# Attention projection of a hybrid encoder: two pairs of token tiles as seven 256-wide products each, with sums of rows kept in the residual tiles

## The reference

```python
h = rms_norm(x, norm_mix_g[l])
u = jnp.einsum('bsd,dc->bsc', h, w_in)         # one projection for four mixers
u_na, u_ml, u_cv, u_at = jnp.split(u, [...], axis=-1)
# u_at: 512 columns: 256 of queries (4 heads), 128 of keys and 128 of values (2 heads)
qd = axial_rope(rms_norm(qd, att_q_norm_g), seq)
kd = axial_rope(rms_norm(kd, att_k_norm_g), seq)
o_at = blocked_gqa(qd, kd, vd)
# ... three other mixers, gates, branch projections, W_out, then x += that
x = x + hierarchical_moe(rms_norm(x, norm_ffn_g[l]), ...)
```

## Time and profile before

| what | value |
|---|---|
| median of 3 runs | 2052.47 us (2051.21 to 2052.56) |
| the profiled execution's own time | 2054.26 us |
| its span (first to last instruction) | 2052.4 us |
| mean granted TensorE clock | 0.986 of full speed |
| PE busy | 1962.9 us, 96% |
| DVE, ACT, POOL busy | 1057.4, 530.5, 388.9 us |
| PE's share of the chain that ended last | 81% |
| head of the first layer, until PE begins the `cv` products | 59.92 us |
| head of the second layer, from PE's first transpose | 1024.88 to 1074.96 us |

### The profile page before, as it was taken

The page is one execution under the profiler, slowest core; times in us unless marked ns, Lnnn a source line. Parts: engine busy times, 40 slices in busy tenths (PEclk is TensorE's granted clock), DMA queues, the critical chain, the costliest instruction groups (busy, mean ns, idle before and its releaser), DMA issues.

```text
span 2052.4 us, 24577 instructions
## 1 busy us (share of the span) xinstructions
PE 1962.9 (96%) x8928; PEld 1263.0 (62%) x8928; DVE 1057.4 (52%) x1895; ACT 530.5 (26%) x1128; POOL 388.9 (19%) x298
## 2 busy tenths in 40 slices
PE   8999999999999999999699999999999999989994
PEld 4555657655556545888445556676656655458882
DVE  3588606554455876111455884255545468651116
ACT  3234312344440001111122332133453300111112
POOL 2322223122120002000323222232112100120013
PEclk9999999999999999999899999999999999999997
DMA  5455668122316505999841111111222183169896
GB/s 212 183 206 200 252 235 319 66 77 88 124 62 250 219 21 215 391 383 375 304 145 74 73 72 72 71 53 62 78 98 108 66 320 145 42 245 424 356 382 243
DMA packets 73400, 375.20 MB, mean 183 GB/s; under 512 B 6289, under 2 KB 8721, under 8 KB 60066
## 3 DMA queue, kind: packets, MB, share of 16 engines
q1 hardware_dynamic: 40818, 259.27, 32.7%
q10 hardware_dynamic: 23824, 82.90, 10.5%
q0 software_dynamic: 8640, 31.46, 4.0%
HBM read 262.41 MB, written 112.25 MB: 183 GB/s over the span
## 4 chain that ended last, share of the span: by engine, by line
PE 81%; DVE 7%; DMA 4%; ACT 3%; issue 2%; POOL 2%; ACTq 0%; DVEq 0%; SPq 0%; POOLq 0%
PE bank L817 35%; PE bank L1761 9%; PE bank L1621 8%; PE bank L1646 5%; PE bank L1796 4%; PE bank L830 3%; PE bank L595 2%; PE bank L795 2%; PE bank L848 2%; PE bank L871 2%; PE bank L927 2%; PE bank L857 2%; DMA blocks<-ring,slots 1%; PE bank L1753 1%; PE bank L912 1%
## 5 line engine op out<-in xcount | busy, mean ns | idle before, releaser
L817 PE MATMUL bank<-hT,ring 128*128 128x384 f32 x1056 | 361.4, 492 | 5.5 <-ACT gbuf L1008 5.5
L817 PE MATMUL bank<-x,ring 128*128 128x384 f32 x1056 | 360.7, 490 | 3.8 <-issue 2.6
L817 PEld LDWEIGHTS bank<-hT,ring 128*128 128x128 f32 x1056 | 196.6, 191 | 152.7 <-issue 31.0
L817 PEld LDWEIGHTS bank<-x,ring 128*128 128x128 f32 x1056 | 194.9, 190 | 146.7 <-issue 26.6
L1187 DVE SCALAR_TENSOR_TENSOR reg_a<-cvx,pp,reg_a 128x783 f32<-128x783 f32 x120 | 141.2, 1177 | 4.3
L981 ACT ACTIVATE sums<-bank 128x384 f32<-128x384 f32 x132 | 64.7, 490 | 289.4 <-PE bank L817 286.9
L1148 DVE SCALAR_TENSOR_TENSOR gbuf<-bank,sums 128x384 f32<-128x384 f32 x96 | 53.5, 558 | 138.5 <-PE bank L817 106.0
L2152 DVE SCALAR_TENSOR_TENSOR prob<-prob,bank 128x256 f32<-128x256 f32 x30 | 12.6, 421 | 180.1 <-ACT prob L1873 180.0
L595 PE MATMUL bank<-ring,hT 128*128 128x512 f32 x192 | 89.2, 620 | 1.6 <-ACT hT L614 1.6
L1841 ACT ACTIVATE prob<-x 128x1024 f32<-128x1024 f32 x12 | 12.7, 1057 | 291.8 <-DVE x L2004 291.8
L1402 POOL TENSOR_TENSOR ring<-cvx,ring 128x512 f32<-128x512 f32 x20 | 25.6, 1282 | 304.8 <-PE bank L817 304.8
(11 more groups left out here) (332 smaller groups left out, 3212.7 us busy)
## 6 DMA issues: line engine op xcount, KB each, us to landing
ring<-in_wd SPq DMA_DIRECT2D x26, 2048.0 KB, 8.5
blocks<-hT SPq DMA_DIRECT2D x16, 3072.0 KB, 20.5
gate_dram<-gbuf ACTq DMA_DIRECT2D x64, 384.0 KB, 2.4
ring<-gate_dram SPq DMA_DIRECT2D x16, 1536.0 KB, 7.6
ring<-in_we SPq DMA_DIRECT2D x8, 2048.0 KB, 13.6
hT<-blocks ACTq DMA_DIRECT2D x26, 512.0 KB, 9.0
wide<-in_we SPq DMA_DIRECT2D x6, 2048.0 KB, 20.2
oT<-in_we SPq DMA_DIRECT2D x6, 2048.0 KB, 18.1
```

Source lines behind the costliest of these rows:

```text
L817: mm = nc.tensor.matmul(bank[i % 2][:, 0:HALF], w[:, k, :], a[:, k, :], start=(k == 0 and r in (0, 1, 3)), stop=(k == 3), skip_group_check ...
```

## The change

Tiles 1 and 2, and tiles 4 and 5, are projected as pairs (`AT_PAIRS`), each in seven products: here the weights' column halves of 256 are what moves, a product has four matmuls of 256 columns (new L629), and r = 0 to 6 take the blocks in the order b11, b21, T2, D, T3, b22, T4. Tiles 0 and 3 stay as they were (new L612). Four sums of weights (D, T2, T3, T4; `weights_sum`, new L760, 128 x 1024 each) are made by DVE into `wide`, four sums of rows for each pair (`rows_sum`, new L769, 128 x 512 each) into the tiles of `x` of the pair itself, once they are scaled. The load of the bias table to `wide` goes behind the second chunk load of `mix_sync`. ACT copies products 0, 2, 3 and 6, DVE adds 1, 4 and 5 (new L777). The sums of rows of the whole for `cv` now wait until product 5 of the second pair is done, since they are written over all of `x`, and piece 2 of part 0 of the rotation stands between the second and the third of them; the other pieces move as well. POOL's powers of the tiles all come ahead of that of the rotation.

```diff
-PROJ_UNITS = {"at": 6, "mo": 6, "mg": 2}
+PROJ_UNITS = {"mo": 6, "mg": 2}
+AT_PAIRS = (1, 4)
...
-    for u in range(PROJ_UNITS["at"]):
-        add("proj", "at", u)
-    add("rope", 1, 0)
+    for t in range(T):
+        if t in AT_PAIRS:
+            for r in range(PRODUCTS):
+                add("proj", "at", t, r)
+        elif t - 1 not in AT_PAIRS:
+            add("proj", "at", t, None)
     for i in range(2 * PRODUCTS):
         product("cv", i // PRODUCTS, i % PRODUCTS)
-        if i in (1, 5):
-            add("rope", 1, 1 + i // 5)
-        if i == 5:
+        if i == 1:
+            add("rope", 0, 3)
+        if i in (2, 4, 6):
+            add("rope", 1, i // 2 - 1)
+        if i == 6:
             add("rope", 1, 3)
...
+            def pair(t, r):
+                i = at["proj", "at", t, r]
+                if r < 2:
+                    pe.wait_ge(ht_ev, 2 * t + 1 + r)
+                else:
+                    pe.wait_ge(s_done, 4 * AT_PAIRS.index(t) + {2: 2, 3: 2, 4: 3, 5: 4, 6: 4}[r])
+                if r == 6:
+                    pe.wait_ge(ht_ev, 2 * t + 4)
+                if i >= 2:
+                    pe.wait_ge(proj_ev[i % 2], i // 2)
+                b, a = ((at_b11, at_q(t, 0)), (at_b21, at_q(t, 1)), (at_t2, at_s(t, 1)), (at_d, at_s(t, 0)),
+                        (at_t3, at_s(t, 2)), (at_b22, at_s(t, 3)), (at_t4, at_q(t + 1, 1)))[r]
+                for k in range(4):
+                    mm = nc.tensor.matmul(bank[i % 2][:, 0:BW], a[:, k, :], b[:, k, :], start=(k == 0 and r in (0, 1, 3)),
+                                          stop=(k == 3), skip_group_check=True)
+                mm.then_inc(proj_mm, 1)
+
+            turn(0)
+            for first in AT_PAIRS:
+                tile(first - 1)
+                turn(first + 1)
+                for r in range(PRODUCTS):
+                    if r == 5 and first + 2 < T:
+                        turn(first + 2)
+                    pair(first, r)
...
             head_square(act, layer, 1)
-            for t in range(1, T):
-                if t + 1 < T:
-                    head_square(act, layer, t + 1)
-                evict(t)
-                project(t - 1)
-            project(T - 1)
+            head_square(act, layer, 2)
+            evict(1)
+            project(0)
+            evict(2)
+            head_square(act, layer, 3)
+            head_square(act, layer, 4)
+            for r in (0, 2, 3):
+                pair(1, r)
+            evict(3)
+            pair(1, 6)
+            head_square(act, layer, 5)
+            evict(4)
+            project(3)
+            evict(5)
+            for r in (0, 2, 3, 6):
+                pair(4, r)
...
+            if layer:
+                for n in range(4):
+                    weights_sum(n)
+                add_late(0)
+                variance(0)
+                scale(0)
+                add_late(1)
+                add_late(2)
+            else:
+                norm(0)
+            norm(1)
+            norm(2)
             if layer == 0:
-                for t in range(T - 1):
-                    variance(t)
-                    scale(t)
...
+                weights_sum(0)
+                weights_sum(1)
+            rows_sum(1, 0)
+            rows_sum(1, 1)
+            pair(1, 1)
+            for n in (2, 3):
+                if layer == 0:
+                    weights_sum(n)
+                rows_sum(1, n)
+            norm(3)
+            pair(1, 4)
+            pair(1, 5)
             dve.wait_ge(consts_done, 16)
             dve.wait_ge(params_in, 32 * (layer + 1))
             rope(dve, done, 0, 0)
-            variance(T - 1)
-            scale(T - 1)
-            for piece in (1, 2, 3):
-                rope(dve, done, 0, piece)
+            norm(4)
+            norm(5)
+            rows_sum(4, 0)
+            rows_sum(4, 1)
+            pair(4, 1)
+            rows_sum(4, 2)
+            rows_sum(4, 3)
+            rope(dve, done, 0, 1)
+            pair(4, 4)
+            pair(4, 5)
             done(ts_(bg_half, pp[:, PP_BG:PP_BG + 32], 0.5, None, ALU.mult), bgh_done)
...
                 if r == 2:
-                    pe.wait_ge(s_done, 4)
+                    pe.wait_ge(s_done, 4 * len(AT_PAIRS) + 4)
...
-            dve.wait_ge(ht_ev, 2 * T)
+            dve.wait_ge(proj_mm, at["proj", "at", AT_PAIRS[-1], PRODUCTS - 2] + 1)
+            done.n[s_done.num] = 4 * len(AT_PAIRS)
             done(tt(s_of[0], quarter[1][0], quarter[1][1], ALU.add), s_done)
             done(tt(s_of[1], s_of[0], quarter[0][0], ALU.subtract), s_done)
+            rope(dve, done, 0, 2)
             done(tt(s_of[2], quarter[0][0], quarter[1][0], ALU.subtract), s_done)
             done(tt(s_of[3], quarter[0][1], s_of[1], ALU.subtract), s_done)
```

More of the change, by code:

```diff
@@ L581, in head_tensor, with tile @@
             pe.wait_ge(ident_in, 16)
-            turn(0)
-            for t in range(T):
+            def tile(t):
+                i = at["proj", "at", t, None]
                 for k in range(KD):
@@ new lines, in pair, with norm @@
+            def pair(t, r):
+                i = at["proj", "at", t, r]
+                dve.wait_ge(proj_mm, i + 1)
+                held = i - 3 if r == 5 else i - 1
+                dve.wait_ge(proj_ev[held % 2], held // 2 + 1)
+                to = {1: atr[:, t, 0:BW], 4: atr[:, t + 1, BW:], 5: atr[:, t, BW:]}[r]
+                tt(to, bank[i % 2][:, 0:BW], sums[:, 1 if r == 5 else 0, 0:BW], ALU.add).then_inc(proj_ev[i % 2], 1)
+                dve.wait_ge(proj_ev[i % 2], i // 2 + 1)
+            def norm(t):
+                variance(t)
+                scale(t)
+                if layer and t + 2 < T:
+                    add_late(t + 2)
```

84 lines of the change are left out of this document (53 added, 31 removed).

## The result

| | before | after |
|---|---|---|
| median of 4 runs of each on one chip | 2052.51 us (2051.21 to 2052.90) | 2067.01 us (2066.81 to 2067.56) |
| the profiled execution: its time, its span | 2054.26, 2052.4 | 2066.81, 2065.0 |
| mean granted TensorE clock | 0.986 | 0.983 |
| PE, DVE, POOL busy | 1962.9, 1057.4, 388.9 us | 1962.8, 1086.0, 381.5 us |

The ratio is 1.0074, with a 95% interval of 1.0061 to 1.0087: 14.5 us slower. PE's busy time did not fall, though it has 6.5 us less to multiply: instructions at the lower clock count longer. What changed is PE's idle time and its clock.

What follows compares the result with a forecast made beforehand. It took PE, busy 96% of the span, as the bound. Terms −0.3 − 1.6 + 10.8 + 3.4 − 1.1 + 0.6 = +11.8 us on the median 2052.47 gave 2064.3 us, range 2056.5 to 2067.5.

Steps and rivals of the forecast that it cites:

- the term of the clock: Behind PE's waits at product 2 of `cv`, the clock falls each time: 1.7 us, 3.4 in all, between 0 and 5.2.
- Head, layer 1: First layer before `cv`: waits of 0.9, 1.4 and 0.7 us take 3.0 of 3.3 saved; `cv` 0.2 to 0.3 earlier.
- a sign of being wrong: The prediction is wrong if waits in the head sum to more than 3 us a layer.
- Head, layer 2: Second layer's head: waits of 0.9 and 0.7 stay, the 1.4 does not; 1.6 us earlier if the layer starts as before.
- The start of layer 2: Sums of weights beside the gathers: shift of the layer's start put at 0, between −1.5 and +2 us.
- my row: Profile row: a gather takes 0.94 us alone, 1.78 when DVE reads two SBUF tensors beside it; trusted over the skill.
- The sums for `cv`: Ahead of product 2 of `cv`, PE waits 5.4 us a layer for late row sums, 10.8 in all; bounds 3.1 and 6.
- rival C: POOL's sums don't hold up DVE's: wait 3.1 us a layer, 2059.7 with the clock's fall, 2056.3 without; chance 0.12.
- Rival B: Late sums with POOL in their way, but no fall of the clock: 2060.9 us; chance 0.18.
- POOL's wait gone: In `cv`, PE's wait of 0.54 us for POOL's sum of weights (L1402) goes in each layer: −1.1.
- product 5's reading: In `cv`, DVE reads product 5 behind a rotation piece awaiting POOL's power, holding PE at the second group: +0.6 in all.
- Rival D: The rotation's power on POOL blocks DVE's scaling of tile 5, whose turning comes 2.8 us late a layer: 2069.9; chance 0.07.

Runs made afterwards that it cites:

- the repeat: The changed kernel unaltered, measured again on the chip of three later kernels: 2065.45 us, ratio 1.0064.
- split waits: The change, but PE waits ahead of each product of the first `cv` group only for the row sums it reads: 2062.24 us, ratio 1.0046.
- the run with POOL waiting: The change, but POOL's two sums of weights for the first `cv` group wait until the four row sums are done: 2061.54 us, ratio 1.0042.
- rotation behind the sums: The change, but piece 2 of the rotation stands behind the fourth sum of rows instead of in the middle: 2062.40 us, ratio 1.0052.
- the filler: The change, with six unused matmuls of 512 columns ahead of product 2 of the first `cv` group: 2060.34 us, ratio 1.0038.
- the own place: The change, but pairs' row sums in free `oT` space, two big sums made before the second pair's product 5 is read, rotation pieces later: 2066.67 us, ratio 1.0063.
- the spread order with the rotation later: The change, but split waits, the last two big sums behind product 1's reading, and the rotation's part 1 behind later product readings: 2056.34 us, ratio 1.0015.
- the kernel with the rotation between: The change, but row sums in `oT`, head waits removed, rotation's part 1 behind the readings of products 4, 5 and 8: 2046.24 us, ratio 0.9972.

## Why the prediction was right or wrong

The direction, the place and the mechanism were right: slower, by a wait of PE for the last sum of rows ahead of product 2 of `cv`, twice, with the fall of the clock behind it. The size was short: +11.8 forecast, +14.5 measured (13.0 in the repeat), at the upper end of the range (the ratio on the first median, 2052.47, gives 2067.7, just past its end). **The step that failed is the term of the clock**, put at 1.7 us a fall and 3.4 in all: it measured 4.83 (4.35 in the repeat). Term by term, by the ledger's +13.1:

- **Head, layer 1** (−0.3): 0.00. The waits came where they were put: 0.5, 1.4 and 0.8 with the restart, against 0.9, 1.4 and 0.7. I had said that the second pair has none; it has 0.19 (0.36 with the restart), as POOL's sums of `prep` stretch a sum of rows to 1.64. The four are 3.1 us with the restarts, nearly all of the pairs' 3.3 (2.35 by the idle times alone); by the former count they are just over the 3 a layer that was named as a sign of being wrong.
- **Head, layer 2** (−1.6): −1.39.
- **The start of layer 2** (0, between −1.5 and +2): within it. PE's idle time ahead of the first transposes is 15.98 us, 0.7 less than before; it is 15.98 to 17.40 over all kernels with the sums of weights there. From the start of the first gather to the first transposes it is 10.16 us, where it was 11.09 before. Here one gather took 1.79, beside the late part's scalar_tensor_tensor (L731), where two were slowed before. The Trainium skill (SBUF — State Buffer, Who interferes with whom) has tensor_tensor of two tensors leave descriptor generation alone; the traces disagree. In the kernel with split waits a gather that began 0.07 us behind the start of a sum of weights took 1.97:

```profile
1020.19 1.22 DVE L760 TENSOR_TENSOR wide<-wide,ring 128x1024 f32<-128x1024 f32 x1
```

```profile
1020.26 1.97 POOL L535 DMA_INDIRECT reg_b<-late_dram,late_slots  x1 [18.57 <-DMA late_dram<-hT]
```

  So my row was the better guide than the rule. At this place of every trace, a gather that runs beside a DVE instruction with two tensors of SBUF, of either kind, ends 0.79 to 0.83 us behind that instruction's end. In the change this costs little, since three gathers happen to begin just ahead of the end of a sum (1.00, 0.95 and 0.96, against 0.94 alone).
- **The sums for `cv`** (10.8): 5.57 + 5.25 = 10.82. POOL's part of it (2.2 a layer forecast) is 1.9, the run with POOL waiting has shown; so rival C is refuted.
- **The clock** (3.4): (4.74 − 2.58) + (5.25 − 2.58) = 4.83; in the repeat (4.36 − 2.58) + (5.15 − 2.58) = 4.35. This is the step that failed. "At 4.51 − 2.82 = 1.7 us" was read behind a wait of 2.06, where the clock stood low for about 3.4 us (1601.1 to 1604.5), all of it while PE worked. Behind 5.57 and 5.25 it stood low for about 6.8 us each time, and PE worked through the last 4.2 and 5.4 of them; half of that, 2.1 and 2.7, is about what the product lost (2.16 and 2.67). In the repeat it was 3.5 us behind the same wait of 5.57, and the product lost 1.78. So one of these four falls cost hardly more than forecast, and a wait of 3.60 (rotation behind the sums) cost the full 2.7: the loss does not grow with the wait. I had kept 5.2 as the bound, and a price between the two would have been nearer. Rival B, no fall, is refuted.
- **POOL's wait gone** (−1.1) and **product 5's reading** (+0.6): together 13.1 + 1.39 − 10.82 − 4.83 = −1.2. The +0.6 did not appear; the slow clock covered it, and with the filler it came at 0.40 in each layer.
- **Rival D** (the rotation's power blocks DVE) is refuted by the first layer: POOL's power runs from 44.21 for 3.22 us, and DVE's scaling beside it takes its usual time.

```profile
44.28 1.28 DVE L753 SCALAR_TENSOR_TENSOR reg_a<-x,small,probT 128x1024 f32<-128x1024 f32 x1 [0.66 <-POOL small L846]
```

- **A slip.** Under the second layer the prediction compares 10.4 with 11.9; its sum is 11.8.
- **The base.** The first comparison lies 1.4 us above the ledger, the second 0.6. No step foresaw it, and it is the rest of the miss. The profiled execution before lies 1.8 us above its median, that after 0.2 below its own. More or fewer falls of the clock elsewhere may be behind it, but that is not shown: outside the counted stretches both profiles have 58.4 us of low clock, and the other executions have no trace.

What the prediction had not seen at all did not show in its number: the moved rotation. I costed its displacement at +0.6 while PE is late; once PE is not, it costs 1.74 + 3.55 us of waits a layer and a fall of the clock, as much as the late sums. And of the seven products' 6.5 us, 4.5 (2.26 a layer) came out in the head once its three waits went.

## What to carry to other kernels

When an order is tightened on an engine that was off the critical path, list what stands behind each of its waits for the case that the bound engine comes in time, not only for the case forecast: a wait that is removed uncovers the next one at its full price. Price a fall of the clock by a range and not by one sighting: in `cv` it took between 1.3 and 2.7 us from the next product, and 1.8 and 2.2 behind the same wait of 5.57.

## What the runs showed of the hardware

- The granted clock at the start of the second layer rises from 0.50 at a moment that differs: the same first six matmuls of 512 columns took 6.79 us with the own place (rise at about 1034.0, PE's first transpose at 1028.51) and 8.32 in the spread order with the rotation later (1034.8 and 1026.14). In the first layer they took 6.79 to 8.45 at a granted clock that the windows show as 1.00, so the cause is open there. Times in a head must be counted from behind them.
- An indirect gather (DMA_INDIRECT on POOL) takes 0.94 us alone. Beside a DVE instruction that reads two tensors of SBUF, at the start of the second layer, it ended 0.79 to 0.83 us behind that instruction's end in all 16 traces, whether tensor_tensor (1.97 us at worst, split waits) or scalar_tensor_tensor (1.98, the kernel before); beside a DVE copy out of PSUM (L2275, the kernel after, 999.33) it took 0.94.
- Beside POOL's sums of weights (tensor_tensor), DVE's tensor_tensor instructions of two SBUF tensors take longer: 2.3 us for the rotation's of 1152 elements where 1.36 is usual, 3.86 to 4.33 for the four where 1.94 is. POOL's sum is sometimes longer too (2.40 us in the kernel with the rotation between) and sometimes hardly (1.43 and 1.27 above). POOL's power of 3.22 us did nothing of the kind to the scaling at 44.28.
- Behind waits of 2.24 us and less in `cv` the clock stayed up, behind 3.23 and more it fell each time; between them it went either way (outside `cv` it fell once behind 2.06), so the same wait of 2.76 was followed by a slow product in the first layer (4.08 us) and by one of 2.75 in the second, in one execution.
